# First product on the undivided input, its weights read a stage ahead, and one unit of gate z moved across a stage boundary

## The reference, cut to what matters

```
for l in range(DEPTH):                      # DEPTH = 2
    h = _rmsnorm(x, mix_norm[l])            # x * rsqrt(mean(x*x) + eps) * w, over 1024 features
    p = h @ w_in[l]
    qkv = silu(_dwconv(qkv, dn_conv))       # 5 taps over the 512 tokens, per channel
    ...                                     # l2 norms of q and k, gates, the delta rule in two directions
    o_dn = _gated_rmsnorm(o_dn, z, dn_norm) # ... * silu(z)
```

## Time and profile before

| | |
|---|---|
| median of 3 runs | 2912.02 us (2911.06 to 2913.5) |
| the profiled execution | 2913.11 us, of which the span from first to last instruction 2911.2 us |
| PE busy | 2788.1 us, 96% of the span |
| DVE, ACT, POOL busy | 51%, 41%, 32% |
| mean granted clock of TensorE | 0.986 of 2.4 GHz |

### The profile page before, as it was taken

How to read it: one execution, slowest core, us unless ns; L and a number is a source line. 1 busy time by engine, 2 the same in 40 slices (tenths; PEclk the granted TensorE clock), 3 DMA queues, 4 the chain that set the end, 5 groups by cost and what they waited for, 6 DMA issues and landing times. The chain is left out here.

```text
span 2911.2 us, 41446 instructions
## 1 busy us (share of the span) xinstructions
PE 2788.1 (96%) x17106; PEld 2282.1 (78%) x17106; DVE 1495.9 (51%) x2092; ACT 1191.1 (41%) x1909; POOL 940.5 (32%) x490
## 2 busy tenths in 40 slices
PE   7999998999999989999989999999899999999999
PEld 5788877888888867888778888888687778888887
DVE  5565656447616455655574476165596552531120
ACT  4563765333312235637552333122344643342231
POOL 1363020014534413630200145444173224344433
PEclk8999999999999999999999999999999999999999
DMA  5102202333323241022023334232522223333332
GB/s 171 54 7 72 73 2 74 98 112 92 115 82 97 70 117 58 3 72 73 2 74 98 112 95 117 78 97 70 134 80 64 72 64 90 97 100 95 95 86 80
DMA packets 414364, 235.85 MB, mean 81 GB/s; under 512 B 24052, under 2 KB 404578, under 8 KB 413538
## 3 DMA queue, kind: packets, MB, share of 16 engines
q1 hardware_dynamic: 413298, 233.18, 27.7%
q10 hardware_dynamic: 880, 0.02, 0.0%
HBM read 226.88 MB, written 6.29 MB: 80 GB/s over the span
## 5 line engine op out<-in xcount | busy, mean ns | idle before, releaser
L2248 POOL TENSOR_TENSOR WLO<-RAW,WHI 128x1024 fp32r<-128x1024 f32 (+1 forms) x199 | 521.9, 2629 | 976.2 <-ACT WHI L2084 976.2
L145 PE MATMUL PS<-HHI,WHI 128*128 128x512 f32 x1920 | 755.4, 393 | 3.2 <-DVE WLO L2927 2.2
L147 PE MATMUL PS<-HHI,WLO 128*128 128x512 f32 x1920 | 748.0, 390 | 0.0
L146 PE MATMUL PS<-HLO,WHI 128*128 128x512 f32 x1920 | 747.9, 390 | 0.0
L2084 ACT CAST WHI<-RAW 128x1024 fp32r<-128x1024 f32 (+1 forms) x202 | 221.5, 1100 | 509.4 <-PE PS L147 496.2
L145 PEld LDWEIGHTS PS<-HHI,WHI 128*128 128x128 f32 x1920 | 360.8, 188 | 87.8 <-issue 7.4
L146 PEld LDWEIGHTS PS<-HLO,WHI 128*128 128x128 f32 x1920 | 360.8, 188 | 75.9 <-issue 2.6
L147 PEld LDWEIGHTS PS<-HHI,WLO 128*128 128x128 f32 x1920 | 360.9, 188 | 75.8
L2237 DVE TENSOR_TENSOR X<-X,PS 128x512 f32<-128x512 f32 x48 | 32.9, 687 | 334.2 <-PE PS L147 334.2
L2220 DVE SCALAR_TENSOR_TENSOR ACC<-GP,PARS,ACC 128x512 f32<-128x512 f32 x88 | 163.1, 1853 | 3.1
L145 PE MATMUL PS<-MHI,WHI 128*128 128x512 f32 x384 | 150.4, 392 | 7.4 <-DVE LHID L2178 4.2
(11 more groups left out here) (493 smaller groups left out, 5156.8 us busy)
## 6 DMA issues: line engine op xcount, KB each, us to landing
RAW<-in_w_up SPq DMA_DIRECT2D x88, 512.0 KB, 3.7
RAW<-in_w_in SPq DMA_DIRECT2D x82, 512.0 KB, 3.8
RAW<-in_w_mlp SPq DMA_DIRECT2D x64, 512.0 KB, 3.9
RAW<-in_w_down SPq DMA_DIRECT2D x32, 704.0 KB, 4.4
RAW<-in_w_in SPq DMA_DIRECT2D x20, 1024.0 KB, 5.0
RAW<-in_w_gate SPq DMA_DIRECT2D x32, 512.0 KB, 4.0
RAW<-in_w_out SPq DMA_DIRECT2D x24, 512.0 KB, 4.8
x_kept<-X SPq DMA_DIRECT2D x2, 2048.0 KB, 9.1
```

The lines of the kernel that those rows point to most:

```text
L145: e.matmul(out, wh, xh, start=first and n == 0, stop=False)
L146: e.matmul(out, wh, xl, start=False, stop=False)
L147: last = e.matmul(out, wl, xh, start=False, stop=final and n == len(quads) - 1)
L2248: pool.tensor_tensor(slot(WLO, u), source(u), slot(WHI, u), ALU.subtract).then_inc(lo_s, 1)
```

## The change

It has four parts. The weights of units 0 to 3 are read by the stage before (at the end of `start_stage` for layer 0, behind the last weight of `out_and_ffn_stage` for layer 1) into a buffer RAWQ of their own, in eight transfers of one k-tile for all four units. The 1408 KB of constants move from `start_stage` into layer 0's `qkv_stage`. The product of units 0 to 3 is made from the undivided input, x times mix_norm, split by ACT (`raw_high`) and DVE (`raw_low`); RS is made meanwhile, and DVE multiplies the four units by it in PSUM ahead of their convolution. The divided input is still made, for the gates and units 4 to 15, into the same HHI and HLO as PE lets go of each k-tile (`u_used`). Last, unit 15 leaves the end of the stage: its split weights lie in OHG (`late`), its 24 matmuls stand at the head of `delta_stage`, ACT copies the result, and its Silu is applied in `hgrn_proj_stage`. Unit 10 also moves ahead of the sums of the l2 norms, and turned keys move behind unit 13.

```diff
-                sp.dma_start(C[:, 2:, :], A["consts"][:, 2:N_KEPT, :]).then_inc(consts_in, 16)
                 sp.wait_ge(cleared, 1)
                 for at, src in loads:
                     n = src.shape[0]
                     sp.dma_start(ROWS[at % P:at % P + n, at // P, :], src).then_inc(rows_in, 16)
-                sp.wait_ge(consts_in, 16)
+                then(sp)
             @block.tensor
             def _(pe):
...
+FIRST_PIECES = ((0, 1), (1, 2), (2, 4), (4, 8))
+def first_weights(sp, A, l, raw, sems):
+    wl = A["w_in"][l].rearrange("(k p) n -> p k n", p=P)
+    for (k0, k1), s in zip(FIRST_PIECES, sems):
+        for k in range(k0, k1):
+            sp.dma_start(raw[:, :, k, :], wl[:, k, 4 * P:8 * P].rearrange("p (u n) -> p u n", n=P)).then_inc(s, 16)
...
+                def raw_high(k):
+                    act.activation(pair[0][:, k, :], X[:, k, :], ACT.Copy, scale=PAR[:, MIX + k:MIX + k + 1]).then_inc(S["u_hi"], 1)
+                def first_high(p):
+                    k0, k1 = pieces[p]
+                    k_first, k_last = FIRST_PIECES[landed_with[p]]
+                    act.wait_ge(first_in[landed_with[p]], 16 * (k_last - k_first))
+                    act.copy(WHI[:, :, k0:k1, :], RAW[:, :, k0:k1, :]).then_inc(S["first_hi"], 1)
+                def normed_high(k):
+                    act.wait_ge(S["x_normed"], k + 1)
+                    act.wait_ge(S["u_used"], k + 1) if k < K - 1 else act.wait_ge(used, 4)
+                    act.copy(pair[0][:, k, :], TK[k % 4]).then_inc(S["x_hi"], 1)
+                first_high(0)
+                raw_high(0)
+                first_high(1)
+                raw_high(1)
+                raw_high(2)
+                first_high(2)
+                raw_high(3)
                 act.wait_ge(S["eps_set"], 1)
-                act.activation(WARM[:, :], EPS[:, :], ACT.Ln).then_inc(S["warm"], 1)
                 act.wait_ge(S["x_sums"], 1)
                 act.activation(RS[:, :], PS[:, 6, :], ACT.Ln, scale=1.0 / (K * P), bias=EPS[:, 0:1]).then_inc(S["x_root"], 1)
                 act.wait_ge(S["x_root"], 1)
                 act.activation(RS[:, :], RS[:, :], ACT.Exp, scale=-0.5).then_inc(S["x_root"], 1)
-                high(0)
-                for k in range(K):
-                    if 0 < k + 1 < N:
-                        high(k + 1)
-                    act.wait_ge(S["x_normed"], k + 1)
-                    act.copy(pair[0][:, k, :], TK[k % 4]).then_inc(S["x_hi"], 1)
+                first_high(3)
+                first_high(4)
+                raw_high(4)
                 act.wait_ge(S["wba_in"], 16)
                 act.copy(WB[:, :, 0:16], WBA[:, :, :]).then_inc(S["wba_hi"], 1)
+                for k in range(K):
+                    normed_high(k)
+                    if k + 5 < K:
...
+                for p, (k0, k1) in enumerate(pieces):
+                    pe.wait_ge(S["first_lo"], p + 1) if p < 3 else pe.wait_ge(S["first_lo_pool"], p - 2)
+                    for k in range(k0, k1):
+                        pe.wait_ge(S["u_lo"], k + 1)
+                        for i in range(4):
+                            last = product(pe, PS[:, i, :], [quad(i, k)], first=k == 0, final=k == K - 1)
+                            if k == K - 1:
+                                last.then_inc(used, 1)
+                        if k < K - 1:
+                            last.then_inc(S["u_used"], 1)
+                pe.wait_ge(S["wba_lo"], 1)
                 for k in range(K):
                     pe.wait_ge(S["x_lo"], k + 1)
-                    for i in range(4):
...
                 for c in range(4):
                     last = pe.matmul(PS[:, 6, c * 16:(c + 1) * 16], BAT[:, tokens(c)], FOLD, start=True, stop=True)
                 last.then_inc(S["ba_turned"], 1)
-                for i in range(5, 10):
+                for i in range(5, 11):
                     dense(i)
                 for n in range(8):
                     unit_sum(n)
-                for i in range(10, 13):
+                for i in range(11, 14):
                     dense(i)
                 for h in range(4):
                     turned_keys(h)
-                dense(13)
                 dense(14)
                 for h in range(4):
                     turned_values(h)
-                dense(15)
             @block.vector
             def _(dve):
...
+                        dve.tensor_tensor(src, src, RS[:, :], ALU.mult).then_inc(S["scaled"], 1)
+                        dve.wait_ge(S["scaled"], i + 1)
                     w = lambda tap: PAR[:, t + tap * 12:t + tap * 12 + 1]
...
+                def raw_low(k):
+                    dve.wait_ge(S["u_hi"], k + 1)
+                    dve.scalar_tensor_tensor(pair[1][:, k, :], X[:, k, :], PAR[:, MIX + k:MIX + k + 1], pair[0][:, k, :], ALU.mult, ALU.subtract).then_inc(S["u_lo"], 1)
+                def first_low(p):
+                    k0, k1 = pieces[p]
+                    dve.wait_ge(S["first_hi"], p + 1)
+                    dve.tensor_tensor(WLO[:, :, k0:k1, :], RAW[:, :, k0:k1, :], WHI[:, :, k0:k1, :], ALU.subtract).then_inc(S["first_lo"], 1)
                 def unit(n):
...
+                first_low(0)
+                raw_low(0)
+                first_low(1)
+                raw_low(1)
+                raw_low(2)
+                first_low(2)
+                raw_low(3)
                 dve.wait_ge(S["x_root"], 2)
                 for k in range(K):
                     if k >= 4:
                         dve.wait_ge(S["x_lo"], k - 3)
                     dve.scalar_tensor_tensor(TK[k % 4], X[:, k, :], PAR[:, MIX + k:MIX + k + 1], RS[:, :], ALU.mult, ALU.mult).then_inc(S["x_normed"], 1)
-                    if k + 1 >= N:
-                        low_of_input(k + 1 - N)
-                        u = k + 1 - N
-                        if u < N:
-                            dve.wait_ge(hi_s, u + 1)
-                            dve.tensor_tensor(WLO[:, u], RAW[:, u], WHI[:, u], ALU.subtract).then_inc(lo_dve, 1)
-                for k in range(K - N + 1, K):
-                    low_of_input(k)
-                dve.wait_ge(S["wba_hi"], 1)
-                dve.tensor_tensor(WB[:, :, 16:32], WBA[:, :, :], WB[:, :, 0:16], ALU.subtract).then_inc(S["wba_lo"], 1)
-                dve.tensor_tensor(FOLD, C[0:32, IDENT, 0:16], C[0:32, IDENT, 16:32], ALU.add).then_inc(S["fold"], 1)
+                    if k + 4 < K:
+                        raw_low(k + 4)
+                    if k:
+                        low_of_input(k - 1)
+                    if k == 4:
...
+                for p in (3, 4):
+                    k0, k1 = pieces[p]
+                    pool.wait_ge(S["first_hi"], p + 1)
+                    pool.tensor_tensor(WLO[:, :, k0:k1, :], RAW[:, :, k0:k1, :], WHI[:, :, k0:k1, :], ALU.subtract).then_inc(S["first_lo_pool"], 1)
                 for u in range(N, T):
-                    pool.wait_ge(hi_s, u + 1)
-                    pool.tensor_tensor(WLO[:, u % N], RAW[:, u % N], WHI[:, u % N], ALU.subtract).then_inc(lo_pool, 1)
+                    pool.wait_ge(hi_s, u - N + 1)
...
+                        pe.wait_ge(S["zc"][0], 1)
                     for h in H4:
...
+                product(pe, bank(0, 2), [(late[0][:, k, :], late[1][:, k, :], pair[0][:, k, :], pair[1][:, k, :]) for k in range(8)]).then_inc(S["z"][0], 1)
...
+                    else:
+                        act.wait_ge(S["z"][0], 1)
+                        act.copy(Z[:, 3, :], bank(0, 2)).then_inc(S["zc"][0], 1)
...
+                       + [f"hi{c}" for c in range(4)] + ["siluz"] + [f"silu{g}_{m}" for g in (3, 4) for m in range(4)])
...
                     sp.dma_start(source(u), units[u][1]).then_inc(raw_in[u % N], 16)
+                if then is not None:
+                    then(sp)
                 if out is not None:
```

105 lines of the change are left out of this document (60 added, 45 removed).

## The result

The changed kernel takes 2894.6 us in the median of four runs (2891.9, 2892.0, 2897.3, 2897.9) against 2912.8 of the kernel before: ratio 0.9939, interval 0.9921 to 0.9956. It is faster, by some 18 us. Forecast were 26, and the time is 0.6 us above the top of the range given. The profiled run is one of the slower two, 2897.93 us (span 2896.1), 15.2 less than the profiled 2913.1 of before. The sum of the prediction is held against this pair, place by place.

A forecast was written before the change was run, and what follows sets the result against it. PE, busy 96% of the span, was taken as the bound. 2.9 + 8.2 + 7.8 + 2 x 4.1 - 2 x 0.2 - 2 x 0.3 = 26.1 us off 2913.1 gives 2887.0, 2886 in the median; range 2880 to 2894.

The forecast's parts named there:

- the start: End of start_stage: without the constants ahead of them the tables land sooner; gain 2.9 us, bounds 0 to 3.8.
- unit 4: In qkv_stage: unit 4 starts 29.3 us (layer 0) and 29.8 us (layer 1) into the stage; gains 8.2 and 7.8.
- Unit 15: End of qkv_stage: 24 matmuls (5.45 us) leave, the tail of 2.35 us is 1.35 longer; net gain 4.1 a layer.
- Head of the delta stage: Start of delta_stage: first level 1.4 us late, about 1.2 of half-clock loss goes; net +0.2 a layer, -0.5 to +1.6.
- First product: Units 0 to 3 in qkv_stage: starts 2.1 us into the stage, does not starve, ends at 24.9 (layer 1: 25.4).
- DVE beside POOL: First product in qkv_stage: POOL's two new rests hold up DVE's loop; 0.3 us a layer charged, between 0 and 2.
- rival 4: First product: DVE and POOL exclude each other whole, PE 1.2 us late in each layer; 2888 us, chance 0.10.
- rival 1: First product: PE starves from k-tile 4 on, rests or weights being late; 2894 us, or 2898; chance 0.12.
- Rival 5: First product: PE stays at 1.2 GHz throughout, waiting in every k-tile; 18 us late a layer, 2922 us, chance 0.02.

The follow-up runs named there:

- not_ahead: The changed kernel without reading ahead: the first four units' weights are issued at the head of qkv_stage in both layers; 2907.2 us, ratio 0.9974.
- z_back: The changed kernel with unit 15 and its Silu put back at the end of qkv_stage; 2897.2 us, ratio 0.9944.
- split_early: The changed kernel with gate z's three Silus before the values' copies and unit 15 split: 2 k-tiles behind the turned values, 6 behind the key products; 2881.7 us.
- early_z_back: The changed kernel with unit 15 back at the end of qkv_stage and gate z's first three Silus ahead of the copies of the values; 2895.7 us.
- dve_rests: The changed kernel with the low parts of the first weights' k-tiles 4 to 7 made by DVE instead of POOL; 2894.9 us, ratio 0.9937.
- tail_fill: The changed kernel with nine unread matmuls behind the turned values, where PE stands still at the end of qkv_stage; 2886.7 us, ratio 0.9907.

## Why the prediction was wrong

The direction held, and the terms of the start, of unit 4 and of unit 15 came out to within 1.1 us each; the sum was 8.6 us too good (11.0 in the profiled pair). The step that failed is the price of the idle tail. "Unit 15" counts the tail of 2.35 us by its length alone, and "Head of the delta stage" reckons the products behind it at full clock: the fall of the clock behind this new gap was put at nothing. It cost 1.4 and 4.4 us.

- **Start.** 2.5 for 2.9. The tables land 2.5 sooner, and their copies still begin 0.3 after the last sum of squares, so the tables still decide. The eight weight transfers took SP 7.9 us instead of 4; without them T is 19.07 (not_ahead), the 19.05 of the prediction. That later transfers of a queue can't pass earlier ones is not what the trace shows: the third weight transfer, issued at 11.82, landed at 16.95, before the first, issued at 10.83, which landed at 17.21.
- **First product.** It starts at T+2.1 as forecast and never starves. The clock was to be low until about T+4.3. In the profiled run it was low until T+6.1, and in layer 1 for 6.8 us, and the product ended 1.0 and 1.1 us later than reckoned. In three other kernels with the same instructions there (z_back, split_early, early_z_back) it was back by T+4.0 in layer 0, and unit 4 came at T+29.2 to 29.3, where 29.3 was forecast. So this miss is chance more than a wrong step. Two slips stand in the working: 25.0 + 0.6 + 1.04 is 26.6 and not 26.8, and the 1 us that it gives layer 1 for the clock is charged by half (24.9 becomes 25.4).
- **DVE beside POOL.** The 0.3 a layer charged, and rival 4's 1.2, were not there: PE has no wait inside the product (dve_rests).
- **Unit 15.** The stage is 3.9 shorter for a forecast 4.1. The tail came out at 2.41 for 2.35.
- **Head of the delta stage.** With the first level 1.4 later the head was to be 10.8 us long; it took 12.2 and 15.2. The small products ahead of unit 15 took 6.5 and 9.4 us instead of 5.1, and as PE goes from them straight to unit 15 and from there to the first level, all of it is lost. The other half of this step was right: the half clock behind the old hole is gone, and 1.0 and 0.9 us came back there for a forecast 1.2. In short, the hole after the key products was closed and a new gap was opened before them, and the text priced the clock of the first and not of the second. tail_fill is the proof: with the gap filled, the head is 10.8 in both layers.
- **The warning in its own rows.** In layer 1 of the kernel before, PE stands still for 2.44 us ahead of the sum of squares, and the clock falls 1.1 us after PE's restart. The prediction used this for the first product and not for the tail of nearly the same length.
- **Behind the first levels.** 2.3 us were lost at no named place, from `hgrn_stage` on in both layers. No run here says why.
- **Rivals.** None of those named came true. The time is near that of rival 1, but its mechanism (the product starves) did not occur. Rival 5 had the right cause, a clock held down by gaps, at the wrong place: it was looked for only in the first product.

With the gap filled by unread work the same change takes 2886.7 us, against the 2886 of the prediction. That is partly chance, as the start and the first product fell short by 2.5 us in the profiled pair and the other stretches' clock varies by as much.

## What to carry to other kernels

When work leaves a place at which it covered other engines' last operations, ask how long PE now stands still there and what it does next. The price of the gap is its length plus some time at half clock behind it (here 2.4 us of gap, and 1.4 to 4.5 us more in the ten heads behind one), and it is paid in full where PE's own instructions set the time. Fill such a gap with part of the work that is moved (a sum in PSUM may be left open across the stage's end), and shorten it by putting ahead what the other engine would do last. Judge steps of a few microseconds by the times of their own stage, since the clock elsewhere moves the total by as much.
